# Decoder trunk on one core: the order of the first loads and casts is changed

## The chip, the core and the metric

The kernel runs on one core of a Trainium2 chip. The core has five engines that each run their own list of instructions in order and wait for one another by semaphores: TensorE (matrix products), VectorE, ScalarE, GpSimd and SyncE, which here does nothing but issue the DMAs. The metric is the device time of one launch in microseconds (us).

## The reference

Two layers over 512 tokens of 1024 features. Layer 0 mixes the tokens by causal forgetting attention (16 heads of 64), layer 1 by a short gated convolution. What the change touches is the start of layer 0:

```python
h = rmsnorm(x, norm_pre[i])                       # fox_mixer:
proj = h @ w_in                                   # columns: q | k | v | z | f
f_logit = proj[..., 4 * ATTN_WIDTH:] + b_f
log_f = jax.nn.log_sigmoid(f_logit)
# fox_attention: c = cumsum(log_f)
# logit[t, s] = q_t.k_s / sqrt(Dh) + c[t] - c[s], causal; softmax; times v
return (o * jax.nn.silu(z)) @ w_out
# then x = x + rmsnorm(y, norm_post[i]); x = x + sigmoid(rmsnorm(x, pe_norm[i]) @ pe_w_gate[i]) * (p[i] @ pe_w_proj[i])
```

## The kernel before

**Numbers in two parts.** Every float32 operand of a large product is split into a high part, rounded to the format that TensorE takes (`act_hi`, `w_hi`, `q_hi` and so on), and a low part, what the rounding left (`act_lo`, `w_lo`). A product is then three matmuls into one PSUM bank: high weight by high activation, high weight by low activation, low weight by high activation (`products`, L1028 to L1030). The features lie on the partitions: x is eight tiles of 128 features by 512 tokens.

**Weights come in slots.** A slot is 128 columns of a weight matrix over all 1024 rows, 512 KB. SyncE loads it into one of two raw buffers (`w_raw`, `load_slot`); ScalarE rounds it to the high part (`weight_hi`, L468); GpSimd subtracts to get the low part in four pieces (`weight_lo`, L408), counts `w_ready` up, and so frees the raw buffer for the slot after the next. High and low parts lie in a ring of four. Slots 0 to 3 are q, k, v and z of the first pair of heads, slots 4 to 7 those of the second pair, and so on.

**The prologue.** For each tile of x ScalarE makes `act_hi` (L487) and some of the squares for the norm (L490), VectorE `act_lo` (L728), the other squares (L732), and sums of two squares (L735). TensorE multiplies each tile by the weights of the forget gates (L1052, L1053) and the squares, singly or as sums of two, by a matrix of 1/1024 for the mean (L1062). The norm's scale `rs` is applied only behind the projections. ScalarE and VectorE then make the running sum of the forget gates; SyncE stores it in HBM and reads it back broadcast over the partitions as `bias` rows, four DMAs for each of the two heads of a pair (`load_bias`, L327). In the prologue the two sets of bias rows are issued with slot 4 between them. TensorE meanwhile projects slots 0 and 1.

**The turns.** A turn of 16 steps projects one pair of heads (4 slots, 4 steps each) and does the attention of the pair before. Turn 0 only projects, and there slots 2 and 3 are left. Every engine has its own written order of the steps. In turn 0: step 2, 6, 10 on ScalarE are `weight_hi` of slots 3, 4, 5, step 14 of slot 6 behind v's high part; steps 4 and 5 are q's high parts (L564), step 8 k's (L570), step 14 v's (L588). VectorE scales q, k and v at steps 4, 8, 12 (L795), with q's and k's low parts between (L824, L832). TensorE transposes v at step 14 (L1037), in the middle of slot 3. From turn 1 on ScalarE also does the exps of the attention (L524), VectorE the logits and the normalisation (L763, L772), GpSimd adds the causal mask to the bias rows (L416) between the slots' low parts. Behind eight turns comes the output projection, the gate of layer 0, the convolution layer and its tail; the change touches none of it.

Of the kernel before, what the change touches and what calls it, by code (L numbers as in the profile page):

```python
# [24 lines left out]
ACT = mybir.ActivationFunctionType  # L25
# [4 lines left out]
KT = D // P  # L30
# [9 lines left out]
RING = 4  # L40
# [8 lines left out]
STEP_QKVZ = 0  # L49
# [32 lines left out]
V_AT = 14  # L82
# [3 lines left out]
NORM_AFTER = KT - 3  # L86
PAIRED = 6
WARM = 11
# [24 lines left out]
def trunk(nc, xT_in, pT_in, weights, f_in, b_f_in, pre_in, post_in, pe_in, taps_in, outT):  # L113
# [6 lines left out]
    with ctx:  # L120
# [192 lines left out]
        def _(sp):  # L313
# [15 lines left out]
            for k in range(KT):  # L329
                sp.dma_start(xT[:, k, :], xT_in[k]).then_inc(x_loaded[k], 16)  # L330
                if k == 0:
                    sp.dma_start(g_pre[:], pre_in).then_inc(g_loaded[0], 16)
                    sp.dma_start(f_raw[:], f_in).then_inc(f_loaded, 16)
                if k == 1:
                    load_slot(0, 0)
            sp.dma_start(b_f[:], b_f_in).then_inc(g_loaded[1], 16)
            for slot in range(1, 4):
                load_slot(slot, slot)
# [3 lines left out]
            sp.wait_ge(negc_stored, 16)  # L342

            load_bias(0, 0)
            load_slot(4, 4)
            load_bias(0, 1)
            sp.dma_start(g_post[:], post_in).then_inc(g_loaded[2], 16)
            sp.dma_start(g_pe[:], pe_in).then_inc(g_loaded[3], 16)
            sp.dma_start(taps[:], taps_in).then_inc(g_loaded[4], 16)
            for slot in range(5, 10):  # L350
                load_slot(slot, slot)
# [35 lines left out]
        def _(pool):  # L387
# [41 lines left out]

            pool.wait_ge(act_ready, KT - 1)  # L430
            for slot in range(3):
# [29 lines left out]
        def _(act):  # L461
# [22 lines left out]
            for k in range(KT):  # L484

                act.wait_ge(x_loaded[k], 16)
                nc.scalar.activation(act_hi[0][:, k, :], xT[:, k, :], ACT.Copy, scale=g_pre[:, 0, k:k + 1]  # L487
                                     ).then_inc(act_hi_done, 1)
                if k % 2 == 0 or k >= PAIRED:
                    nc.scalar.activation(x_sq[k][:], xT[:, k, :], ACT.Square).then_inc(x_sq_act, 1)  # L490
                if k == 1:
                    weight_hi(0, 0)
            weight_hi(1, 1)

# [20 lines left out]
            act.wait_ge(f_act, 2)  # L515
            nc.scalar.activation(f_ln[:], f_ln[:], ACT.Ln, bias=1.0).then_inc(f_act, 1)
            weight_hi(2, 2)
            nc.scalar.preload_act_table(ACT.Tanh)

# [25 lines left out]
            def turn(m0, jj, project, attend):  # L545
# [3 lines left out]
                for g in range(GROUPS):  # L549
# [22 lines left out]
                    if g == WEIGHTS_AT and not project:  # L572
                        weight_hi(SLOT_OUT[0] + 3, SLOT_OUT[0] + 3)
                    if g % 4 == WEIGHTS_AT and project and (attend or g != V_AT):

                        weight_hi(count(3 + g // 4, 4, m0, jj), 3 + 4 * m0 + g // 4)
                    if attend and g in SUM_AT:
                        head_half(SUM_AT[g], m0, jj)
                    if g == V_AT and project:
# [144 lines left out]
        def _(dve):  # L724
            for k in range(KT):
# [295 lines left out]
        def _(pe):  # L1021
# [28 lines left out]
            for k in range(KT):  # L1050
# [4 lines left out]
                if k == KT - 1:  # L1055
                    end.then_inc(f_done, 1)
                if k >= PAIRED:
                    pe.wait_ge(x_sq_act, PAIRED // 2 + k - PAIRED + 1)
                elif k % 2 == 1:
                    pe.wait_ge(x_pair, k // 2 + 1)  # L1060
                if k >= PAIRED or k % 2 == 1:
                    end = nc.tensor.matmul(ps_o[:], mean_f[:], x_sq[k][:], start=k == 1, stop=k == KT - 1)  # L1062
            end.then_inc(ms_done, 1)

            bank = ps_pj[STEP_QKVZ % 2]
            pe.wait_ge(w_hi_done, SLOT_QKVZ + 1)
            for k in range(KT):
                w_h = w_hi[SLOT_QKVZ % RING][:, k, :]
                nc.tensor.matmul(bank[:], w_h, act_hi[0][:, k, :], start=k == 0, stop=False)
                nc.tensor.matmul(bank[:], w_h, act_lo[0][:, k, :], start=False, stop=False)  # L1070
            pe.wait_ge(w_ready, SLOT_QKVZ + 1)
            for k in range(KT):
                end = nc.tensor.matmul(bank[:], w_lo[SLOT_QKVZ % RING][:, k, :], act_hi[0][:, k, :], start=False,
                                       stop=k == KT - 1)
# [212 lines left out]
```

## Time and profile before

| | us |
|---|---|
| median of 3 runs | 659.37 (658.58 to 660.58) |
| the profiled execution, own time | 658.61 |
| its span, first to last instruction | 656.8 |
| TensorE busy in it | 635.0 (97%) |
| VectorE, ScalarE, GpSimd busy | 389.9, 321.2, 308.1 |

Times in the rows are us from the start of the span. Matmuls overlap in the pipeline: one of 128x512 is shown with some 0.39 us, and the next starts 0.23 us behind it. The share of a whole engine is an average; the places where TensorE is not busy have to be read stretch by stretch.

### The profile page before, as it was taken

To read this page: it belongs to the slowest core of one execution; us is meant where nothing else is said; L and a number is where in the kernel's file an instruction comes from. 1 tells how busy PE (TensorE), PEld (TensorE's weight loads), DVE (VectorE), ACT (ScalarE), POOL (GpSimd) and SP (SyncE) were. 2 spreads that over 40 slices of the span, in tenths; PEclk is the share of its full clock that TensorE was granted. 3 is DMA by queue.
4 is the path that set the end of the run, shared out by engine and by line. 5 is a ranking of instruction groups with operands and counts; after the bars stand their busy time and mean duration, and the time that the engine had idled before them with its cause. 6 is when DMAs were issued, how large, how long until landed. Compare 5 with 4: busy or idle time off the path is not lost.

```text
span 656.8 us, 9280 instructions
## 1 busy us (share of the span) xinstructions
PE 635.0 (97%) x2930; PEld 516.4 (79%) x2930; DVE 389.9 (59%) x776; ACT 321.2 (49%) x556; POOL 308.1 (47%) x412
## 2 busy tenths in 40 slices
PE   6979999999999999899989999999999999999897
PEld 3758888888888887788767778888888887887686
DVE  5528787867878787645678735333423343365864
ACT  6536575755656575465547633212222222465461
POOL 1765555556464445200277647547454752001770
PEclk9989999999999999999999999999999999999999
DMA  6253333332433333135002413232223232250041
GB/s 200 88 174 128 127 106 105 104 105 104 129 118 114 111 129 125 33 128 188 6 33 72 150 53 110 98 125 96 96 68 123 96 128 87 94 173 32 33 128 65
DMA packets 27161, 68.69 MB, mean 105 GB/s; under 512 B 3568, under 2 KB 10096, under 8 KB 27136
## 3 DMA queue, kind: packets, MB, share of 16 engines
q1 hardware_dynamic: 27136, 68.37, 31.6%
q8 instruction: 14, 0.23, 0.1%
q14 instruction: 11, 0.09, 0.0%
HBM read 66.23 MB, written 2.13 MB: 104 GB/s over the span
## 4 chain that ended last, share of the span: by engine, by line
PE 81%; DVE 9%; ACT 4%; issue 3%; DMA 2%; SPq 0%; DVEq 0%; ACTq 0%
PE ps_pj L1028 23%; PE ps_pj L1030 23%; PE ps_pj L1029 23%; PE ps_tr L1037 3%; DVE act_lo L918 2%; DMA w_raw<-in_weights 2%; PE ps_o L1141 1%; PE ps_o L1142 1%; DVE xT L914 1%; PE ps_sc L1111 1%; PE ps_sc L1109 1%; PE ps_tr L1028 1%; PE ps_tr L1030 1%; PE ps_tr L1029 1%; ACT logit L524 1%
## 5 line engine op out<-in xcount | busy, mean ns | idle before, releaser
L408 POOL TENSOR_TENSOR w_lo<-w_raw,w_hi 128x256 fp32r<-128x256 f32 x324 | 251.5, 809 | 138.5 <-ACT w_hi L468 128.3
L1028 PE MATMUL ps_pj<-act_hi,w_hi 128*128 128x512 f32 (+1 forms) x736 | 293.9, 399 | 5.5 <-DVE act_lo L918 4.4
L1030 PE MATMUL ps_pj<-act_hi,w_lo 128*128 128x512 f32 (+1 forms) x736 | 286.2, 389 | 0.0
L1029 PE MATMUL ps_pj<-act_lo,w_hi 128*128 128x512 f32 (+1 forms) x736 | 285.9, 388 | 0.0
L1028 PEld LDWEIGHTS ps_pj<-act_hi,w_hi 128*128 128x128 f32 x736 | 138.8, 189 | 37.2 <-DVE act_lo L918 7.9
L1030 PEld LDWEIGHTS ps_pj<-act_hi,w_lo 128*128 128x128 f32 x736 | 138.5, 188 | 29.3
L1029 PEld LDWEIGHTS ps_pj<-act_lo,w_hi 128*128 128x128 f32 x736 | 139.0, 189 | 24.9 <-issue 0.7
L468 ACT CAST w_hi<-w_raw 128x1024 fp32r<-128x1024 f32 x96 | 100.6, 1048 | 97.4 <-DMA w_raw<-in_weights 74.9
L443 POOL TENSOR_TENSOR acc<-acc,sq 128x512 f32<-128x512 f32 x14 | 21.4, 1525 | 118.5 <-ACT sq L616 117.6
L416 POOL TENSOR_TENSOR bias<-bias,future 128x128 f32<-128x128 f32 x64 | 34.0, 562 | 72.8 <-DMA bias<-negc_scratch 72.8
L524 ACT ACTIVATE logit<-logit,nmax 128x128 f32<-128x128 f32 (+1 forms) x64 | 36.1, 564 | 60.4 <-DVE nmax L763 60.2
L778 DVE TENSOR_TENSOR pt_lo<-ps_tr,pt_hi 128x128 fp32r<-128x128 f32 (+1 forms) x64 | 30.7, 483 | 8.1 <-ACT pt_hi L534 7.1
L772 DVE TENSOR_SCALAR logit<-logit,rrec 128x128 f32<-128x128 f32 (+1 forms) x64 | 32.6, 510 | 2.2
L891 DVE TENSOR_TENSOR w_lo<-w_raw,w_hi 128x1024 fp32r<-128x1024 f32 x15 | 18.4, 1225 | 25.5 <-ACT w_hi L468 25.5
L763 DVE CUSTOM_DVE_ANT_0 logit<-ps_sc,bias 128x128 f32<-128x128 f32 (+1 forms) x64 | 31.0, 484 | 0.3
L1037 PE MATMUL ps_tr<-ident,logit 128*128 128x128 f32 x160 | 28.2, 274 | 2.3 <-DVE logit L772 2.2
L1037 PEld LDWEIGHTS ps_tr<-ident,logit 128*128 128x128 f32 x160 | 20.5, 140 | 10.3 <-DVE logit L772 4.2
L1005 DVE TENSOR_TENSOR cv_z<-ps_pj,rs 128x512 f32<-128x512 f32 x8 | 5.5, 691 | 38.0 <-PE ps_pj L1030 38.0
L534 ACT CAST pt_hi<-ps_tr 128x128 fp32r<-128x128 f32 (+1 forms) x64 | 26.4, 423 | 2.4 <-PE ps_tr L1037 1.3
L824 DVE TENSOR_TENSOR q_lo<-scaled,q_hi 64x512 fp32r<-64x512 f32 x32 | 24.8, 776 | 3.4 <-ACT q_hi L564 3.0
L985 DVE TENSOR_TENSOR cv_w<-ps_pj,cv_c 128x512 f32<-128x512 f32 x8 | 5.5, 691 | 31.6 <-PE ps_pj L1030 31.4
L918 DVE SCALAR_TENSOR_TENSOR act_lo<-xT,g_pe,act_hi 128x512 fp32r<-128x512 f32 x16 | 20.9, 1318 | 5.2 <-ACT act_hi L655 5.2
(143 smaller groups left out, 724.8 us busy)
## 6 DMA issues: line engine op xcount, KB each, us to landing
w_raw<-in_weights SPq DMA_DIRECT2D x100, 512.0 KB, 3.4
bias<-negc_scratch SPq DMA_DIRECT2D x16, 256.0 KB, 7.4
bias<-negc_scratch SPq DMA_DIRECT2D x16, 192.0 KB, 6.1
xT<-in_xT SPq DMA_DIRECT2D x8, 256.0 KB, 5.5
bias<-negc_scratch SPq DMA_DIRECT2D x16, 128.0 KB, 4.8
out<-xT SPq DMA_DIRECT2D x7, 256.0 KB, 2.0
bias<-negc_scratch SPq DMA_DIRECT2D x16, 64.0 KB, 3.4
p_in<-in_pT SPq DMA_DIRECT2D x2, 512.0 KB, 4.5
```

The costliest lines, as they stand in the source:

```text
L408: last = nc.gpsimd.tensor_tensor(w_lo[place % RING][:, tiles], w_raw[stream(place) % RAW][:, tiles], w_hi[place % RING][:, tiles], ALU.sub ...
L416: nc.gpsimd.tensor_tensor(diagonal, diagonal, future[:], ALU.add).then_inc(bias_ready[h], 1)
L468: nc.scalar.copy(w_hi[place % RING][:], w_raw[position % RAW][:]).then_inc(w_hi_done, 1)
L524: nc.scalar.activation(logit[b][:, 0:n], logit[b][:, 0:n], ACT.Exp, scale=-1.0, bias=nmax[:, b:b + 1], accum_out=rsum[:, b:b + 1]).then_in ...
L763: nc.vector.tensor_tensor_reduce(out=logit[b][:, 0:n], in0=ps_sc[u % 2][:, 0:n], in1=bias[h][:, i, 0:n], scale=-1.0, scalar=3e38, op0=ALU. ...
L772: nc.vector.tensor_scalar(logit[b][:, 0:n], logit[b][:, 0:n], rrec[:, b:b + 1], None, ALU.mult).then_inc(prob_ready, 1)
L778: nc.vector.tensor_tensor(causal(pt_lo, i), ps_tr[n % TR_BANKS][:, 0:(i + 1) * P].rearrange("p (k c) -> p k c", c=P), causal(pt_hi, i), AL ...
L918: nc.vector.scalar_tensor_tensor(a_g[1][:, m - 1, :], xT[:, m - 1, :], g_pe[:, l, m - 1:m], a_g[0][:, m - 1, :], ALU.mult, ALU.subtract).t ...
L1028: nc.tensor.matmul(out, w_h, a[0][:, k, tokens], start=k == first, stop=False)
L1029: nc.tensor.matmul(out, w_h, a[1][:, k, tokens], start=False, stop=False)
L1030: end = nc.tensor.matmul(out, w_l, a[0][:, k, tokens], start=False, stop=k == last)
L1037: last = nc.tensor.transpose(ps_tr[n % TR_BANKS][:, t * P:(t + 1) * P], tile, ident[:])
```

## The change

SyncE issues the eight tiles of x first, then the forget bias, then slots 0 to 3; slot 0 stood behind tile 1. Behind the store of the forget sums, slot 4 is issued ahead of the first set of bias rows, and slots 5 and 6 between the two sets; 4 stood between the sets, and 5 and 6 behind both. ScalarE squares tiles 0, 1, 2, 4, 6 and 7 and VectorE tiles 3 and 5 (before, VectorE had 1, 3 and 5), so that TensorE's mean has six products and not five. `weight_hi` of slot 0 goes behind all of x, that of slot 1 behind the norm's scale, that of slot 2 behind the load of the tanh table. In turn 0, q's, k's and v's high parts go ahead of slot 3, of slot 4 and of slots 5 and 6. GpSimd's first low part waits for eight tiles of `act_lo` and not seven. TensorE projects slot 1 as it did slot 0: all products with the high part first, then those with the low part.

```diff
-PAIRED = 6
+PAIRED = {2: 3, 4: 5}
+MEANS = [k for k in range(KT) if k not in PAIRED]
+TURN_0_WEIGHTS = {5: [0], 8: [1], 14: [2, 3]}
@@ SyncE
-                if k == 1:
-                    load_slot(0, 0)
             sp.dma_start(b_f[:], b_f_in).then_inc(g_loaded[1], 16)
-            for slot in range(1, 4):
+            for slot in range(4):
                 load_slot(slot, slot)
...
+            load_slot(4, 4)
             load_bias(0, 0)
-            load_slot(4, 4)
+            load_slot(5, 5)
+            load_slot(6, 6)
             load_bias(0, 1)
...
-            for slot in range(5, 10):
+            for slot in range(7, 10):
                 load_slot(slot, slot)
@@ GpSimd
-            pool.wait_ge(act_ready, KT - 1)
+            pool.wait_ge(act_ready, KT)
@@ ScalarE
-                if k % 2 == 0 or k >= PAIRED:
+                if k not in PAIRED.values():
                     nc.scalar.activation(x_sq[k][:], xT[:, k, :], ACT.Square).then_inc(x_sq_act, 1)
-                if k == 1:
-                    weight_hi(0, 0)
-            weight_hi(1, 1)
+            weight_hi(0, 0)
...
             norm_scale(0, rs[:])
+            weight_hi(1, 1)
...
+            nc.scalar.preload_act_table(ACT.Tanh)
             weight_hi(2, 2)
-            nc.scalar.preload_act_table(ACT.Tanh)
...
-                    if g % 4 == WEIGHTS_AT and project and (attend or g != V_AT):
+                    if g % 4 == WEIGHTS_AT and project and attend:
...
-                        if not attend:
-                            weight_hi(3 + g // 4, 3 + g // 4)
+                    if not attend:
+                        for j in TURN_0_WEIGHTS.get(g, []):
+                            weight_hi(3 + j, 3 + j)
@@ VectorE
-                if k % 2 == 1 and k < PAIRED:
+                if k in PAIRED.values():
@@ TensorE (the second slot of the first projection)
-            pe.wait_ge(w_ready, SLOT_QKVZ + 2)
-            for k in range(KT):
-                end = products(ps_pj[(STEP_QKVZ + 1) % 2], SLOT_QKVZ + 1, act0, [k], 0, KT - 1)
+            for j in range(2):
+                bank, place = ps_pj[(STEP_QKVZ + j) % 2], (SLOT_QKVZ + j) % RING
+                pe.wait_ge(w_hi_done, SLOT_QKVZ + j + 1)
...
+                pe.wait_ge(w_ready, SLOT_QKVZ + j + 1)
```

SyncE behind the first four slots, before. `w_raw0` and `w_raw1` are the two raw buffers, and the number behind `bias` is the head of the pair:

```order
L341 DMA negc_scratch<-f_abs 16x512 [waits f_chain]
L327 DMA bias0<-negc_scratch 128x128 [waits negc_stored]
L327 DMA bias0<-negc_scratch 128x256
L327 DMA bias0<-negc_scratch 128x384
L327 DMA bias0<-negc_scratch 128x512
L319 DMA w_raw0<-in_weights 128x1024 [waits w_ready]
L327 DMA bias1<-negc_scratch 128x128
```

and now:

```order
L341 DMA negc_scratch<-f_abs 16x512 [waits f_chain]
L321 DMA w_raw0<-in_weights 128x1024 [waits w_ready,negc_stored]
L329 DMA bias0<-negc_scratch 128x128
L329 DMA bias0<-negc_scratch 128x256
L329 DMA bias0<-negc_scratch 128x384
L329 DMA bias0<-negc_scratch 128x512
L321 DMA w_raw1<-in_weights 128x1024 [waits w_ready]
L321 DMA w_raw0<-in_weights 128x1024 [waits w_ready]
L329 DMA bias1<-negc_scratch 128x128
```

Slot 4 (the first `w_raw0` of each) moved from behind four bias rows to ahead of them, and slots 5 and 6 came in ahead of the second set.

ScalarE before, from where the norm's scale `rs` is made. `w_hi0` stands for slots 0, 4, 8, `w_hi1` for slots 1, 5 and so on:

```order
L500 ACTIVATE rs<-ln_ms 128x512 [waits ln_done]
L512 ACTIVATE f_abs<-f_x1,b_f 16x512 [waits f_scaled,g_loaded1]
L514 ACTIVATE f_ln<-f_abs 16x512 [waits f_act]
L516 ACTIVATE f_ln<-f_ln 16x512 [waits f_act]
L468 CAST w_hi2<-w_raw0 128x1024 [waits w_loaded0]
L518 ACT_TABLE_LOAD
L468 CAST w_hi3<-w_raw1 128x1024 [waits w_loaded1]
L564 CAST q_hi00<-scaled0 64x512 [waits pj_free0]
...
L468 CAST w_hi0<-w_raw0 128x1024 [waits pj_done,w_loaded0]
L570 CAST k_st00<-scaled1 64x512 [waits pj_free1]
L570 CAST k_st01<-scaled1 64x512
```

and now:

```order
L500 ACTIVATE rs<-ln_ms 128x512 [waits ln_done]
L470 CAST w_hi1<-w_raw1 128x1024 [waits w_loaded1]
...
L518 ACT_TABLE_LOAD
L470 CAST w_hi2<-w_raw0 128x1024 [waits w_loaded0]
L565 CAST q_hi00<-scaled0 64x512 [waits pj_free0]
...
L470 CAST w_hi3<-w_raw1 128x1024 [waits w_loaded1]
L571 CAST k_st00<-scaled1 64x512 [waits pj_free1]
L571 CAST k_st01<-scaled1 64x512
L470 CAST w_hi0<-w_raw0 128x1024 [waits pj_done,w_loaded0]
```

The cast of slot 4 (`w_hi0` here) moved from ahead of k's high parts to behind them, slot 3's from ahead of q's to behind, and the table load from behind slot 2's cast to ahead of it.

## Rows read from the trace of the kernel before

**Rows 1.** Windows of TensorE: stretch, length, busy (instructions), granted clock, DMA share, GB/s.
```profile
38.20:42.30 4.10, 0.00 (x0) 1.00 0.77 184
42.30:46.00 3.70, 3.67 (x11) 0.54 0.41 149
...
47.20:255.00 207.80, 207.63 (x1061) 1.00 0.35 114
```

**Rows 2.** Waits of TensorE, all of the span: us in total, times, longest.
```profile
PE ps_tr L1037 <- DVE scaled L795: 4.1, 1, 4.1
```

**Rows 3.** Chain of work that ended last: start us, us, what.
```profile
24.70 2.83 DMA negc_scratch<-f_abs
...
29.34 7.97 DMA w_raw<-in_weights
```

**Rows 4.** Timeline of TensorE: start us, us, instruction.
```profile
18.57 0.80 PE L1069 MATMUL ps_pj<-act_hi,w_hi 128*128 128x512 f32 x1
...
29.88 0.39 PE L1028 MATMUL ps_pj<-act_hi,w_hi 128*128 128x512 f32 x1
...
37.81 0.39 PE L1030 MATMUL ps_pj<-act_hi,w_lo 128*128 128x512 f32 x1
42.33 0.90 PE L1037 MATMUL ps_tr<-ident,scaled 128*128 128x128 f32 x4 [4.13 <-DVE scaled L795]
...
47.19 0.22 PE L1109 MATMUL ps_sc<-k_st,q_hi 128*128 128x128 f32 x1
...
52.13 0.27 PE L1037 MATMUL ps_tr<-ident,logit 128*128 128x128 f32 x1
...
73.74 0.62 PE L1037 MATMUL ps_tr<-ident,scaled 128*128 128x128 f32 x4
...
76.94 0.22 PE L1109 MATMUL ps_sc<-k_st,q_hi 128*128 128x128 f32 x1
```

**Rows 5.** Timeline of ScalarE; in brackets, idle time before and its releaser.
```profile
4.83 0.72 ACT L487 ACTIVATE act_hi<-xT,g_pre 128x512 fp32r<-128x512 f32 x1
...
5.98 0.71 ACT L487 ACTIVATE act_hi<-xT,g_pre 128x512 fp32r<-128x512 f32 x1
7.59 1.05 ACT L468 CAST w_hi<-w_raw 128x1024 fp32r<-128x1024 f32 x1 [0.91 <-DMA w_raw<-in_weights]
8.54 0.72 ACT L487 ACTIVATE act_hi<-xT,g_pre 128x512 fp32r<-128x512 f32 x1
...
23.27 1.03 ACT L468 CAST w_hi<-w_raw 128x1024 fp32r<-128x1024 f32 x1
...
48.33 0.40 ACT L524 ACTIVATE logit<-logit,nmax 128x128 f32<-128x128 f32 x1 [1.85 <-DVE nmax L763]
...
52.80 1.04 ACT L468 CAST w_hi<-w_raw 128x1024 fp32r<-128x1024 f32 x1
...
345.68 1.28 ACT L678 ACT_TABLE_LOAD   x1
346.98 0.63 ACT L698 ACTIVATE t_b<-t_a 128x512 f32<-128x512 f32 x1
```

**Rows 6.** Timeline of VectorE.
```profile
15.22 1.41 DVE L728 SCALAR_TENSOR_TENSOR act_lo<-xT,g_pre,act_hi 128x512 fp32r<-128x512 f32 x2
...
49.06 0.86 DVE L772 TENSOR_SCALAR logit<-logit,rrec 128x128 f32<-128x128 f32 x1
```

**Rows 7.** Timeline of GpSimd.
```profile
24.37 6.62 POOL L408 TENSOR_TENSOR w_lo<-w_raw,w_hi 128x256 fp32r<-128x256 f32 x8 [1.68 <-ACT w_hi L468]
38.47 3.67 POOL L408 TENSOR_TENSOR w_lo<-w_raw,w_hi 128x256 fp32r<-128x256 f32 x4 [7.48 <-ACT w_hi L468]
```

**Rows 8.** DMAs issued at 3.07, 57.0 and 58 to 59.5: KB, us to landing.
```profile
xT<-in_xT SPq DMA_DIRECT2D x1, 256.0 KB, 5.2
...
w_raw<-in_weights SPq DMA_DIRECT2D x1, 512.0 KB, 3.5
...
bias<-negc_scratch SPq DMA_DIRECT2D x1, 256.0 KB, 6.8
```

**Rows 9.** Windows of the DMA engines: stretch, length, clock, share, GB/s.
```profile
8.00:9.00 1.00, 1.00 1.02 365
```

More of the change, by code:

```diff
@@ L730, in _ @@
                                                ).then_inc(act_ready, 1)
-                if k % 2 == 1 and k < PAIRED:
+                if k in PAIRED.values():
+                    pair = list(PAIRED.values()).index(k)
                     nc.vector.tensor_tensor(x_sq[k][:], xT[:, k, :], xT[:, k, :], ALU.mult).then_inc(x_sq_dve, 1)
-                    dve.wait_ge(x_sq_act, k // 2 + 1)
-                    dve.wait_ge(x_sq_dve, k // 2 + 1)
+                    dve.wait_ge(x_sq_act, k - pair)
+                    dve.wait_ge(x_sq_dve, pair + 1)
                     nc.vector.tensor_tensor(x_sq[k][:], x_sq[k - 1][:], x_sq[k][:], ALU.add).then_inc(x_pair, 1)
@@ L1056, in _ @@
                     end.then_inc(f_done, 1)
[L1057 to L1062, printed above, removed]
-            end.then_inc(ms_done, 1)
-            bank = ps_pj[STEP_QKVZ % 2]
-            pe.wait_ge(w_hi_done, SLOT_QKVZ + 1)
@@ L1067, in _ @@
-            for k in range(KT):
[L1068 to L1074, printed above, removed]
@@ L1075, in _ @@
-            end.then_inc(pj_done, 1)
-            pe.wait_ge(w_ready, SLOT_QKVZ + 2)
-            for k in range(KT):
-                end = products(ps_pj[(STEP_QKVZ + 1) % 2], SLOT_QKVZ + 1, act0, [k], 0, KT - 1)
-            end.then_inc(pj_done, 1)
+                summed = sum(paired < k for paired in PAIRED.values())
+                if k in PAIRED.values():
+                    pe.wait_ge(x_pair, summed + 1)
+                elif k not in PAIRED:
+                    pe.wait_ge(x_sq_act, k - summed + 1)
@@ new lines, in _ @@
+                if k in MEANS:
+                    end = nc.tensor.matmul(ps_o[:], mean_f[:], x_sq[k][:], start=k == MEANS[0], stop=k == KT - 1)
+            end.then_inc(ms_done, 1)
+            for j in range(2):
+                bank, place = ps_pj[(STEP_QKVZ + j) % 2], (SLOT_QKVZ + j) % RING
+                pe.wait_ge(w_hi_done, SLOT_QKVZ + j + 1)
+                for k in range(KT):
+                    nc.tensor.matmul(bank[:], w_hi[place][:, k, :], act_hi[0][:, k, :], start=k == 0, stop=False)
+                    nc.tensor.matmul(bank[:], w_hi[place][:, k, :], act_lo[0][:, k, :], start=False, stop=False)
+                pe.wait_ge(w_ready, SLOT_QKVZ + j + 1)
+                for k in range(KT):
+                    end = nc.tensor.matmul(bank[:], w_lo[place][:, k, :], act_hi[0][:, k, :], start=False,
+                                           stop=k == KT - 1)
+                end.then_inc(pj_done, 1)
```

## The prediction

> **What bounds the kernel now.** Read the windows of TensorE first. From 47.2 to 255 us it is busy for 207.63 of 207.80 us [rows 1], so in the attention turns nothing but TensorE's own work sets the time. What an edit of the prologue can gain is what lies in front of 47.2 us, and it is kept if the turns behind stay full. Next the list of TensorE's waits: one entry stands out, 4.1 us before the four transposes of v [rows 2]. The windows around it show nothing running from 38.2 to 42.3, and then a granted clock of 0.54 from 42.3 to 46.0, that is mostly 1.2 GHz where 2.4 had been granted [rows 1]. So the gap costs twice: by itself, and by half speed behind it.
>
> Then the chain, to see what the gap waited for. It runs through the load of the raw weights of slot 4, 7.97 us from issue at 29.34 to landing [rows 3]. ScalarE's order has w_hi of slot 4 ahead of k's high parts; VectorE makes k's low parts before it scales v; TensorE needs scaled v for its transposes. A weight that is first used in turn 1 thereby holds a step of turn 0. In the same place of turn 1 a weight load that has no bias rows ahead of it lands in 3.5 us, and the bias rows issued behind it in 6.8 [rows 8].
>
> The start of the stream is a second place. ScalarE is idle 0.91 us at 7.59, waiting for slot 0's weights, then rounds them for 0.95 us while x tile 2 waits [rows 5]; everything up to TensorE's first projection at 18.57 [rows 4] hangs on this.
>
> **The change part by part.**
>
> *x first, six squares on ScalarE.* Before, ScalarE reaches tile 2 at 8.54. A tile's high part and its square take it 1.15 us (tile 0: 4.83 to tile 1 at 5.98 [rows 5]). After, tile 1 has both, and ScalarE is at tile 2 at 5.98 + 1.15 = 7.12. From tile 2 to 7 the order on ScalarE and VectorE is the same before and after (pairs 2/3 and 4/5 stay on VectorE), so tiles 2 to 7 come **1.42 us** earlier. The pair 0/1 leaves VectorE, two instructions fewer; TensorE has one mean product more, at about 8 us, where it waits for tiles anyway: nothing. The loads must keep up: x tile 2, issued at 3.07, landed 5.2 later, at 8.3 [rows 8]; half a MB of weights less ahead of it is 1.4 us at 365 GB/s [rows 9], so 6.9, in time for 7.12. The tiles behind it come 0.7 us apart at that rate and ScalarE needs 0.9 for one. Slot 0's weights come last, by about 11.6, and are wanted at 12.9 (behind tile 7) and by TensorE at 17.1. The last two act_lo, 15.22 to 16.63 [rows 6], end at 15.2; there GpSimd, which now waits for the eighth instead of the seventh, begins slot 0's low part, done by 18.6 and wanted at 21.2. First projection: 18.57 − 1.42 = 17.15.
>
> *w_hi of slot 1 behind the norm's scale, table load ahead of w_hi 2.* The casts use no time of TensorE as long as they are there: slot 1's high part is wanted at 23.0 and is ready by 20.0; its low part is wanted 16 products later, at 26.6 (this is what the split of slot 1 into high then low products is for), and is ready by 23.4. In the forget gates' chain w_hi 1 fits into a wait for VectorE; I add 0.1 at most. Behind that chain's last activation w_hi 2 started at 23.27 [rows 5]; ScalarE is now there at 21.95. Then the table load comes first, 1.30: w_hi 2 starts at 23.25, as before, while TensorE is 1.42 early: slot 2 started at 29.88 [rows 4], after 28.46. GpSimd's four subtractions for slot 2 start at 24.3. Eight of them at 24.37 took 6.62, so four 3.3; beside VectorE's work on k four took 3.67 [rows 7], and q's low parts now run beside them from 25.6. I take 3.6, near the slower row: ready at 27.9, **margin 0.6 us**, cost nothing. Between 3.3 and 3.67 (27.6 to 28.0) it stays nothing; 4.1 would still fit.
>
> Here a rule speaks against the change. The rows: an activation behind a table load starts 1.30 us after the load does, 345.68 to 346.98 [rows 5]. The Trainium skill (ScalarE: Activation LUTs, "What ACT_TABLE_LOAD costs") gives 1.28 for the load and 1.38 for a drain, 2.66 in all; by that rule slot 2's low part would be ready 1.36 later and TensorE would stand still for 0.8. The trace does not agree with it, and the sum goes by the row.
>
> *Slot 3 and q.* w_hi 3 now comes behind q's high parts, at 26.7, when its load lands too (GpSimd frees the buffer at about 23.4). Its low part is done at about 31.4 and wanted at 33.9.
>
> *Slot 4 ahead of the bias rows.* SyncE's store of the forget sums took 2.83 us from 24.70 to landing [rows 3]; after, it goes out at about 23.8, behind slot 3's load, and is done by 27. Slot 4 waits for GpSimd's slot 2, 27.9, so the bias rows are issued from 28.35, 0.8 later than before. They are first wanted in turn 1. Slot 4 lands at 27.9 + 3.5 = 31.4. k's high parts need it no more: they stand ahead, at 30.2, when VectorE is through with q's low parts and scales k. k's low parts end by 33.5, v is scaled at 34.6 and TensorE wants it at 38.04 − 1.42 = 36.6 (last product 37.81 + 0.23 [rows 4]). **The wait at 42.33 is gone**: 42.33 − 38.04 = 4.29. From the first transpose to the first score of the next turn it is 47.19 − 42.33 = 4.86 us at half speed, and in turn 1, warm, 76.94 − 73.74 = 3.20 [rows 4]: **1.66** more.
>
> *What is late next.* Slots 5 and 6 are now rounded one after the other behind v's high parts, ahead of turn 1's first exp. Slot 5 is issued at about 31.4 behind bias row 0, which by the turn 1 pattern lands 6.8 after its last issue at 29.7 [rows 8]: 36.5, and the weights 1.4 behind, 37.9; v is through at 37.8. Slot 6 waits for slot 4's subtractions (w_hi 31.4 to 32.4, 3.67 for four: 36.1) and lands 3.5 behind that at 39.6. w_hi 6 ends at 40.6. Turn 1 begins at 36.6 + 3.2 = 39.8, and its first exp is wanted 1.14 later (48.33 − 47.19), at 40.95 [rows 5]. It fits by 0.3. Behind it, slot 7 is issued at 42.2 behind bias row 1 and lands at about 45.4, where ScalarE wants it at 52.80 − 7.4 = 45.4 [rows 5]. If one is late, TensorE has slack: the first probabilities, done at 49.92 [rows 6], are taken at 52.13 [rows 4]: 2.2 us.
>
> **The sum.** 1.42 + 4.29 + 1.66 = 7.4 us. The profiled execution took 658.6 us at a span of 656.8, and its span becomes **649.4**, its own time 651.2. The median of the runs shown, 659.37, lies 0.8 above it: forecast **651.9**. All that is behind 47.2 only moves.
>
> **The rivals.** *A. The stall moves to turn 1.* Slots 5, 6 or 7 come later, because each now stands behind a set of bias rows with a slow read; slot 4, in that place, took 8 us. If slot 7 takes 8 from 42.2 it lands at 50.2 and not 45.4; of that TensorE's slack takes some 2, and 2.8 us remain, up to 1.7 more if the clock falls as it did behind 4.1 us of nothing: 654.7 to 656.4. Against it: in turn 1 the order weights, bias, weights shows no TensorE wait.
> *B. The x tiles don't come sooner.* If the weights weren't what delayed them, ScalarE has tile 2 only at 8.3 and the first term shrinks to 0.2: 653.1. For it, a tile takes 5.2 us to land even at a high rate; against it, slot 0's half MB lies ahead of tile 2 in the order of issue.
> *C. Slot 2's low part is late.* The table load holds w_hi 2 for its own length, 1.28, once more; ready at 29.2 and not 27.9, a stall of 0.7: 652.6. Against it: 345.68 to 346.98 [rows 5]. This is the drain of the Trainium skill's page named above.
> *D. Slower.* w_hi 6 stands ahead of the first exp on ScalarE, and nothing passes it. Were slot 6 so late that turn 1 stood still for longer than was gained, the kernel would lose: w_hi 6 has to end 2.2 + 7.4 + 2 − 1.7 = 9.9 us behind 40.95, so slot 6 would have to land at 49.8, 13.7 us after its issue, for 661.4. The load of slot 4 took 7.97 [rows 3].
> *E. The change does nothing*: v still waits, say because bias rows issued later hold slot 4; only if the loads don't start in the order of issue. Gain 1.4, 658.0.
>
> **How the numbers follow.** Forecast with all three terms, 0.68 (that includes C's small stalls up to 0.3); A 0.14; B 0.07; C 0.07; D 0.02; E 0.02. The range from 650.6 (0.5 below the sum for the spread of the runs and a clock that recovers sooner, and 0.8 for a prologue that moves more than 1.42) to 655.2 holds the forecast, B, C and the lower part of A. About 0.3%, 2 us, is what a measurement of this kernel can tell from no change. Faster by more than that: forecast, B, C and nearly all of A, 0.94; within it: E and the worst of A, 0.04; slower: D, 0.02.
>
> **What the profile after would show.** TensorE's first projection at 17.1 to 17.2; slot 2 without a wait at 28.5; no entry of 4 us before the transposes of v, which start at 36.6; a granted clock of 1.00 throughout 38 to 46; turn 1's first score at 39.8; slot 4 landing within 4 us, slots 5 and 6 by 38.5 and 40. A would show as a wait of TensorE at the transposes of turn 1 behind w_hi 6 or 7 that waits for a load; B as ScalarE idle on x tiles; C as a wait at slot 2's first product. I am wrong if turns behind 47.2 show gaps that they did not have, or if another wait takes the place at 36.6.

## The result and the profile after

The changed kernel takes **652.09 us** (median of 4 runs, 651.79 to 652.51) against 659.35 us for the kernel before (4 runs, 658.58 to 660.58) on the same chip: a ratio of 0.9885, with a 95% interval of 0.9862 to 0.9907. The profiled execution took 651.79 us at a span of 650.0.

The windows of TensorE come first again (stretch, length, busy and instructions, granted clock, DMA share, GB/s). They answer to [rows 1]:

```profile
38.20:46.00 7.80, 7.80 (x39) 1.00 0.74 189
40.00:248.00 208.00, 207.27 (x1058) 1.00 0.38 116
```

Where TensorE did nothing for 4.1 us and then ran at a clock of 0.54, it is now busy throughout at 1.00. But the long stretch behind it, which was full to 0.17 us, now has 0.73 us of nothing in it. In the list of TensorE's waits the entry before the transposes of v [rows 2] is gone; of those behind the prologue these are left (us in total, times, longest):

```profile
PE ps_pj L1031 <- DVE act_lo L921: 4.4, 6, 1.1
PE ps_tr L1040 <- DVE logit L775: 2.3, 3, 0.9
```

TensorE's timeline has the first projection, slot 2, the transposes of v and the first scores of turns 1 and 2, for which [rows 4] has 18.57, 29.88, 42.33, 47.19 and 76.94:

```profile
17.35 0.80 PE L1073 MATMUL ps_pj<-act_hi,w_hi 128*128 128x512 f32 x1
...
28.66 0.39 PE L1031 MATMUL ps_pj<-act_hi,w_hi 128*128 128x512 f32 x1
...
36.82 0.60 PE L1040 MATMUL ps_tr<-ident,scaled 128*128 128x128 f32 x4
...
40.01 0.22 PE L1109 MATMUL ps_sc<-k_st,q_hi 128*128 128x128 f32 x1
...
62.82 0.66 PE L1040 MATMUL ps_tr<-ident,logit 128*128 128x128 f32 x4 [0.48 <-DVE logit L775]
...
66.47 0.50 PE L1141 MATMUL ps_o<-pt_hi,v_st 128*128 128x512 f32 x1 [0.23 <-DVE pt_lo L781]
...
71.00 0.22 PE L1109 MATMUL ps_sc<-k_st,q_hi 128*128 128x128 f32 x1
```

Turn 1 starts 7.18 us earlier, turn 2 only 5.94. The 1.24 between them is lost late in turn 1, at the two waits in brackets: compared with the kernel before, each counted from the turn's first score, TensorE is 0.03 behind just ahead of the first and 1.2 behind after the second. The brackets hold 0.71 of it, the rest is the slower run of the matmuls on either side of a wait. ScalarE's timeline shows what the engine waits for on the way there (answering to [rows 5]):

```profile
7.34 0.71 ACT L489 ACTIVATE act_hi<-xT,g_pre 128x512 fp32r<-128x512 f32 x1
...
22.12 1.28 ACT L518 ACT_TABLE_LOAD   x1
...
23.42 1.05 ACT L470 CAST w_hi<-w_raw 128x1024 fp32r<-128x1024 f32 x1
...
39.44 1.05 ACT L470 CAST w_hi<-w_raw 128x1024 fp32r<-128x1024 f32 x1 [1.33 <-DMA w_raw<-in_weights]
40.72 1.05 ACT L470 CAST w_hi<-w_raw 128x1024 fp32r<-128x1024 f32 x1 [0.24 <-DMA w_raw<-in_weights]
41.67 0.40 ACT L525 ACTIVATE logit<-logit,nmax 128x128 f32<-128x128 f32 x1
...
47.11 1.06 ACT L470 CAST w_hi<-w_raw 128x1024 fp32r<-128x1024 f32 x1 [0.95 <-DMA w_raw<-in_weights]
```

The casts of slots 5, 6 and 7 (39.44, 40.72, 47.11) each wait for a load. SyncE's issues show what stands ahead of them (start, length of the group of issues; the two of the last row start at 31.99 and 36.11):

```profile
24.53 0.43 SPq L341 DMA_DIRECT2D negc_scratch<-f_abs  x1
28.36 0.33 SPq L321 DMA_DIRECT2D w_raw<-in_weights  x1
28.73 1.85 SPq L329 DMA_DIRECT2D bias<-negc_scratch  x4
31.99 4.45 SPq L321 DMA_DIRECT2D w_raw<-in_weights  x2
```

Slot 4, with nothing ahead of it, landed 3.2 us behind its issue; slot 5, behind the four DMAs of the first set of bias rows, 7.4. The last of these four took, in KB and us from issue to landing:

```profile
bias<-negc_scratch SPq DMA_DIRECT2D x1, 256.0 KB, 8.0
```

It was issued at 30.15 and landed at 38.11, and slot 5 landed 1.3 behind it, at 39.41.

**A measure that is cleaner than the median.** In what follows each kernel's start is read at two landmarks, the first score of turn 1 and that of turn 2, and the rest is the span less the second. All come from the timelines and spans of the profiled executions, one for each kernel. None of these edits touches anything in the rest. The landmark has its own noise: the change, profiled twice, has turn 2 at 71.00 and at 70.38, and the kernel of e7 and e11 at 70.31 and 70.56. So a difference under some 0.6 us at turn 2 is not shown by one trace of each. The kernel before was profiled once.

| kernel | median | before, same chip | turn 1 at | turn 2 at | rest |
|---|---|---|---|---|---|
| before | 659.35 | | 47.19 | 76.94 | 579.9 |
| the change | 652.09 | 659.35 | 40.01 | 71.00 | 579.0 |
| e1 loads only | 651.40 | 657.27 | 41.60 | 71.38 | 578.4 |
| e2 casts only | 655.41 | 657.27 | 41.12 | 73.93 | 579.7 |
| e3 loads and casts | 651.88 | 657.27 | 41.15 | 71.11 | 579.4 |
| e4 start only | 658.39 | 657.27 | 47.32 | 77.07 | 578.7 |
| e5 gap filled | 655.50 | 658.12 | 45.23 | 74.95 | 578.2 |
| e6 table load behind | 651.77 | 658.12 | 40.02 | 70.57 | 579.6 |
| e7 slot 1 early | 651.57 | 658.12 | 39.81 | 70.31 | 578.4 |
| e8 only slot 4 ahead | 654.80 | 658.12 | 40.11 | 75.00 | 578.6 |
| e9 start and loads | 651.68 | 657.59 | 41.84 | 71.56 | 579.6 |
| e10 the change again | 651.90 | 657.59 | 39.84 | 70.38 | 578.4 |
| e11 slot 1 early again | 651.11 | 657.59 | 39.89 | 70.56 | 578.6 |
| e12 start, slot 1 early | 656.77 | 657.59 | 46.35 | 76.10 | 578.3 |

The rest differs by up to 1.7 us between executions that do the same work there. One part of that is where the attention ends. TensorE's timeline and windows there in e9 (rest 579.6), then the windows in e7 (rest 578.4):

```profile
256.06 0.55 PE L1038 MATMUL ps_tr<-ident,logit 128*128 128x128 f32 x3 [0.90 <-DVE logit L773]
258.46 1.11 PE L1038 MATMUL ps_tr<-ident,logit 128*128 128x128 f32 x4 [1.16 <-DVE logit L773]
```

```profile
256.00:260.00 4.00, 2.79 (x13) 0.79 0.01 2
260.00:264.00 4.00, 4.00 (x17) 0.78 0.37 131
...
258.50:261.50 3.00, 3.00 (x11) 0.50 0.16 41
```

```profile
256.00:260.00 4.00, 2.85 (x18) 1.00 0.10 17
260.00:264.00 4.00, 4.00 (x23) 1.00 0.29 114
```

Both kernels wait there; in some executions the clock falls behind the waits and in others it doesn't. The 0.79 and 0.78 are one fall, seen in two windows: between 258.5 and 261.5 the clock is 0.50, that is 1.2 GHz. Of the six longest rests, e3, e6 and e9 (579.4 to 579.6) have such a fall; before, the change and e2 (579.0 to 579.9) don't. These three are slower in the turns: from the first score of turn 2 to that of turn 8 it takes 179.15, 178.74 and 179.59 us, and 178.3 to 178.5 in the other eleven. The runs of the kernel before that stand beside e9 and e10 have spans of 654.3 to 656.7, on the whole the longer the lower their mean clock (0.997 down to 0.991). So medians tell apart some 1 to 2 us, and only the landmarks can speak of less.

### The profile page after: what moved, and what is told of

Its sections match the earlier page's. It is cut to its first block, busy times and chain, and to the rows that moved or that the text cites. A ratio compares the mean times of both kernels' runs of the same rounds, so it can differ in the third digit from the quotient of the medians.

```text
span 650.0 us, 9283 instructions
## 1 busy us (share of the span) xinstructions
PE 633.4 (97%) x2932; PEld 515.5 (79%) x2932; DVE 388.8 (60%) x774; ACT 321.3 (49%) x557; POOL 308.0 (47%) x412
## 4 chain that ended last, share of the span: by engine, by line
PE 81%; DVE 8%; ACT 3%; issue 3%; POOL 3%; DMA 1%; SPq 0%; DVEq 0%; POOLq 0%; ACTq 0%
PE ps_pj L1031 23%; PE ps_pj L1033 23%; PE ps_pj L1032 23%; PE ps_tr L1040 3%; POOL w_lo L410 2%; DVE act_lo L921 2%; PE ps_o L1141 1%; PE ps_o L1142 1%; DVE xT L917 1%; PE ps_sc L1111 1%; PE ps_sc L1109 1%; PE ps_tr L1031 1%; PE ps_tr L1033 1%; PE ps_tr L1032 1%; ACT logit L525 1%
## 5 line engine op out<-in xcount | busy, mean ns | idle before, releaser
L1031 PE MATMUL ps_pj<-act_hi,w_hi 128*128 128x512 f32 (+1 forms) x728 | 290.0, 398 | 5.5 <-DVE act_lo L921 4.4
L1033 PE MATMUL ps_pj<-act_hi,w_lo 128*128 128x512 f32 (+1 forms) x728 | 282.6, 388 | 0.0
L1032 PE MATMUL ps_pj<-act_lo,w_hi 128*128 128x512 f32 (+1 forms) x728 | 282.3, 388 | 0.0
L1031 PEld LDWEIGHTS ps_pj<-act_hi,w_hi 128*128 128x128 f32 x728 | 136.8, 188 | 36.7 <-DVE act_lo L921 7.9
L1033 PEld LDWEIGHTS ps_pj<-act_hi,w_lo 128*128 128x128 f32 x728 | 136.7, 188 | 28.6
L1032 PEld LDWEIGHTS ps_pj<-act_lo,w_hi 128*128 128x128 f32 x728 | 137.0, 188 | 24.7 <-issue 0.7
```

Source lines behind the costliest of these rows:

```text
L1031: nc.tensor.matmul(out, w_h, a[0][:, k, tokens], start=k == first, stop=False)
L1032: nc.tensor.matmul(out, w_h, a[1][:, k, tokens], start=False, stop=False)
L1033: end = nc.tensor.matmul(out, w_l, a[0][:, k, tokens], start=False, stop=k == last)
```

## The experiments

**e1: only SyncE's order behind the forget sums.** Against the kernel before:

```
-            load_bias(0, 0)
             load_slot(4, 4)
+            load_bias(0, 0)
+            load_slot(5, 5)
+            load_slot(6, 6)
             load_bias(0, 1)
...
-            for slot in range(5, 10):
+            for slot in range(7, 10):
```

> The kernel before, with only the loads of slots 4 to 6 reordered (slot 4 ahead of the first bias rows, 5 and 6 between the sets); casts and prologue as before. Theory: slot 4's late load is what held k's high parts, so the wait before v's transposes goes even with the old cast order: slot 4 lands at about 31, v is scaled at 36.9, wanted at 38.04. Gain 4.3 + 1.7 = 6.0 us, time 653.4, turn 1's first score at 41.2. Rival (the cast order is what counts, a load in front of k's casts still holds them): a wait of 1 us or more remains before v's transposes, time over 655.

651.40 us (4 runs) against 657.27 (16 runs), ratio 0.9912 (0.9897 to 0.9927). TensorE's transposes of v start at 38.41 without a wait, though ScalarE still rounds slot 4 ahead of k's high parts:

```profile
31.44 1.05 ACT L470 CAST w_hi<-w_raw 128x1024 fp32r<-128x1024 f32 x1 [1.61 <-DMA w_raw<-in_weights]
33.52 1.25 ACT L572 CAST k_st<-scaled 64x512 fp32r<-64x512 f32 x2 [1.02 <-DVE scaled L797]
38.99 1.05 ACT L470 CAST w_hi<-w_raw 128x1024 fp32r<-128x1024 f32 x1 [4.23 <-DMA w_raw<-in_weights]
```

Slot 4 was there at 31.4, and k's high parts wait for VectorE and no longer for a load. Moving the three loads is enough by itself. The gain was put at 6.0 us and is 5.9.

**e2: only ScalarE's order in turn 0**, with the loads as late as before. Against the kernel before:

```
+TURN_0_WEIGHTS = {5: [0], 8: [1], 14: [2, 3]}
-                    if g % 4 == WEIGHTS_AT and project and (attend or g != V_AT):
+                    if g % 4 == WEIGHTS_AT and project and attend:
-                        if not attend:
-                            weight_hi(3 + g // 4, 3 + g // 4)
+                    if not attend:
+                        for j in TURN_0_WEIGHTS.get(g, []):
+                            weight_hi(3 + j, 3 + j)
```

> The kernel before, with only turn 0's casts reordered on ScalarE (q, k, v ahead of slots 3, 4, 5 and 6); loads and prologue as before. Theory: the wait before v's transposes goes too (k is cast at 33), but slots 4 to 6 land as late as before (37.3, 43, 45), so slot 4's low part is 0.7 us late for turn 1 and slot 6's cast holds the first exp by some 4 us, of which 2.2 are slack: a gain of 6.0 less 2.6, time 656, more if the clock falls again. Rival (only the cast order matters): 653.4.

655.41 us (5 runs) against 657.27, ratio 0.9966 (0.9953 to 0.9979). The wait at v is gone here too (37.94), and turn 1 starts at 41.12, but the weights come as late as before. ScalarE, casts of slots 4, 5, 6:

```profile
36.86 1.05 ACT L469 CAST w_hi<-w_raw 128x1024 fp32r<-128x1024 f32 x1 [4.92 <-DMA w_raw<-in_weights]
...
42.47 1.05 ACT L469 CAST w_hi<-w_raw 128x1024 fp32r<-128x1024 f32 x1 [3.25 <-DMA w_raw<-in_weights]
43.95 1.05 ACT L469 CAST w_hi<-w_raw 128x1024 fp32r<-128x1024 f32 x1 [0.44 <-DMA w_raw<-in_weights]
```

Slot 6 is rounded until 45.0, ahead of turn 1's first exp, and turn 1 takes 32.81 us from first score to first score where before took 29.75. Of 6.1 us gained at turn 1, half is paid back: this is rival A, in a kernel where it does happen. Slot 4's low part was expected 0.7 us late for turn 1; no such wait shows. At turn 2 the trace is 3.0 us ahead of before; the medians, 1.9 apart, show less, and this execution's rest is among the longest.

**e3: both**, that is the change without its new start.

> The kernel before with both reorderings of turn 0 (loads of slots 4 to 6 and casts), the prologue as before, which is the change without its start. Theory: 6.0 us, time 653.4, the same as the loads alone. Rival (both orders are needed): at least 1 us below the kernel with the loads alone.

651.88 us (4 runs), ratio 0.9915 (0.99 to 0.9931): the same as e1. In the trace turn 2 starts at 71.11, 0.27 earlier than in e1, which is within the noise of the landmark.

**e4: only the new start** (turn 0's loads and casts as before). Against the change:

```
-            load_slot(4, 4)
             load_bias(0, 0)
-            load_slot(5, 5)
-            load_slot(6, 6)
+            load_slot(4, 4)
             load_bias(0, 1)
...
-            for slot in range(7, 10):
+            for slot in range(5, 10):
```

and e2's edit undone.

> The kernel after with turn 0's loads and casts put back as before, so only the start is changed (x first, six squares, places of the casts of slots 0 to 2 and of the table load, slot 1's products). Additive theory: TensorE's first projection at 17.35 and 1.2 us gained at the end, time 658.1. Rival: the end of the wait at v hangs on SyncE's store of the forget sums, which stands behind slot 3's load and so goes out only 0.2 us earlier; then TensorE comes 1.2 us earlier and waits 1.0 longer: gain 0.2, time 659.1, wait at v of about 5.1.

658.39 us (11 runs), ratio 1.0015 (1.0006 to 1.0024): no gain at all, rather 1.1 us lost. SyncE's list of e4, and below it TensorE's wait:

```profile
18.70 6.18 SPq L320 DMA_DIRECT2D w_raw<-in_weights  x2
24.93 0.43 SPq L340 DMA_DIRECT2D negc_scratch<-f_abs  x1
28.02 1.75 SPq L328 DMA_DIRECT2D bias<-negc_scratch  x4
29.82 0.43 SPq L320 DMA_DIRECT2D w_raw<-in_weights  x1
```

```profile
42.48 0.77 PE L1036 MATMUL ps_tr<-ident,scaled 128*128 128x128 f32 x4 [4.64 <-DVE scaled L794]
```

TensorE starts its first projection at 17.74, 0.83 us earlier than before, and waits 0.5 longer for v, which is scaled no sooner. The store of the forget sums stands behind slot 3's load, which needs slot 1's raw buffer free; slot 1 is now rounded behind the norm's scale, so the store still goes out at 24.9 (24.70 before, [rows 3]), the bias rows at 28.0, slot 4 at 29.8.

**e12: e4 with slot 1 rounded right behind slot 0**, to test that reading. Against e4:

```
             weight_hi(0, 0)
+            weight_hi(1, 1)
...
             norm_scale(0, rs[:])
-            weight_hi(1, 1)
```

> Only the start changed, as in the run of the start alone, but slot 1's cast directly behind slot 0's. Theory: the start alone gave nothing because slot 1's low part ended at 24.5, slot 3's load and the store of the forget sums behind it left late (24.93) and the bias rows at 28.02, so v was released no sooner; now the store leaves at 23.5, bias rows at 26.4, v's transposes start near 41.1: 1.2 us below the kernel before. Rival (the start gives nothing for another reason): no gain again.

656.77 us (11 runs) against 657.59 (15 runs), ratio 0.999 (0.998 to 1.0). The store goes out at 24.09, the bias rows at 26.93, v's transposes start at 41.50 and turn 1 at 46.35, 0.97 earlier than in e4. That fits the chain from slot 1's buffer to slot 4; by time it is worth 0.8 of a microsecond and not the 1.2 expected, at the edge of what the runs tell apart.

**e5: the wait stays, the idleness goes.** The kernel before, with 17 matmuls that nothing reads, ahead of v's transposes (added work: its output is not part of the result).

```
                     if g == V_AT and project:
+                        if not attend:
+                            for _ in range(17):
+                                nc.tensor.matmul(ps_tr[1][:], w_hi[3][:, 0, :], act_hi[0][:, 0, :], start=True, stop=True)
```

> The kernel before with 17 matmuls of 128x512 into an unused bank ahead of turn 0's transposes of v (17 x 0.227 = 3.9 us of the 4.3 us gap); their result is used nowhere. Theory: the wait itself stays, the clock does not fall behind it: granted clock 1.00 from 42 to 46, turn 1's first score 1.7 us earlier (45.5), time 657.7. Rival (the slow stretch has another cause than the idle time): no change, 659.4.

655.50 us (7 runs) against 658.12 (10 runs), ratio 0.9968 (0.9948 to 0.9987). A kernel with more work is faster. TensorE's timeline, then the window behind the gap, of e5 and of before:

```profile
37.79 4.01 PE L1094 MATMUL ps_tr<-act_hi,w_hi 128*128 128x512 f32 x17
41.97 0.66 PE L1037 MATMUL ps_tr<-ident,scaled 128*128 128x128 f32 x4 [0.17 <-DVE scaled L795]
...
45.23 0.22 PE L1112 MATMUL ps_sc<-k_st,q_hi 128*128 128x128 f32 x1
```

```profile
42.00:46.00 4.00, 4.00 (x21) 1.00 0.42 131
```

```profile
42.00:46.00 4.00, 3.67 (x11) 0.57 0.40 145
```

In the same 4 us, 21 matmuls at a clock of 1.00 and 11 at 0.57. From the first transpose of v to turn 1's first score it takes 45.23 − 41.97 = 3.26 us, against 4.86 in before [rows 4]: the clock costs 1.60 us, and the forecast had 1.66. (Turn 2 starts 1.99 earlier; 0.36 of it is that v is transposed earlier in this execution. The medians are 2.6 apart, 0.9 more than was expected; what the 0.6 beyond the trace are is open.) This execution has a fall of its own that before doesn't have, in the prologue:

```profile
8.00:12.00 4.00, 3.28 (x7) 0.68 1.02 396
```

The idle times of TensorE ahead of it, 0.39, 0.37 and 0.72 us, are those of the kernel before (0.50, 0.38 and 0.72), where the clock stayed at 1.00. So the length of the stop alone doesn't tell whether the clock falls.

**e6: the table load behind slot 2's cast.** Against the change:

```
-            nc.scalar.preload_act_table(ACT.Tanh)
             weight_hi(2, 2)
+            nc.scalar.preload_act_table(ACT.Tanh)
```

> The kernel after with the tanh table's load put back behind slot 2's cast. Theory: slot 2's low part is ready 0.4 us ahead of TensorE in the kernel after, so an earlier cast gives nothing: 652.1, slot 2's subtractions at 24.2 and not 24.54, since slot 1's end there. Rival (the load costs TensorE something where it stands): over 0.5 us faster.

651.77 us (4 runs), ratio 0.99 (0.9881 to 0.9919); turn 2 at 70.57. The place of the table load makes no difference that the runs can show.

**e7 and e11: the change with slot 1 rounded early** (e12's edit, made in the changed kernel).

> The kernel after with slot 1's cast directly behind slot 0's, where ScalarE is idle from 14.1 to 17.1. Theory: GpSimd ends slot 1 at 21.5 and not 24.1, slot 3 lands at about 25 and not 27.5, the store goes out 0.9 earlier, slot 5 is issued 0.4 us earlier; the waits of ScalarE for slots 5 to 7 shrink, and the 0.7 us that TensorE loses at the end of turn 1 go in part: 0.3 to 0.7 us faster, 651.4 to 651.8. Rival (these waits are all within slack): 652.1.

> The kernel after with slot 1's cast directly behind slot 0's, on the same chip as the kernel after. Theory: 0.3 to 0.7 us faster than it, the 0.5 and 0.2 us waits in turn 1 gone. Rival: no difference.

651.57 us (4 runs) against 658.12, ratio 0.9899 (0.988 to 0.9917), and on another chip 651.11 (4 runs) against 657.59, ratio 0.9907 (0.9889 to 0.9924), beside the change itself (e10) at 651.90. The store goes out at 23.46 in e7, but slot 4 at 28.38 and no sooner, since its raw buffer has to be freed by slot 2's subtractions, and turn 2 starts at 70.31 and 70.56 against 70.38 in e10. The medians lean by 0.8 us to the edit, the landmarks by nothing: not shown to be better.

**e8: only slot 4 ahead of the bias rows**, slots 5 and 6 behind both sets. Against the change:

```
             load_bias(0, 0)
-            load_slot(5, 5)
-            load_slot(6, 6)
             load_bias(0, 1)
...
-            for slot in range(7, 10):
+            for slot in range(5, 10):
```

> The kernel after with slots 5 and 6 loaded behind both sets of bias rows, as before the change; only slot 4 stands ahead. Theory: slot 5 lands near 44 and slot 6 near 46, ScalarE has to cast both ahead of turn 1's first exp, wanted at 41; with 2.2 us of slack TensorE stands still for about 3 us in turn 1, more with the clock: 655 to 657. Rival (only slot 4's place mattered): 652.1.

654.80 us (4 runs) against 658.12, ratio 0.9945 (0.9926 to 0.9964): half of the gain. Turn 1 starts as early as in the change (40.11), and then the first probabilities are late. ScalarE's casts of slots 5 and 6, and TensorE's first transposes of turn 1:

```profile
43.82 1.05 ACT L468 CAST w_hi<-w_raw 128x1024 fp32r<-128x1024 f32 x1 [5.61 <-DMA w_raw<-in_weights]
45.10 1.04 ACT L468 CAST w_hi<-w_raw 128x1024 fp32r<-128x1024 f32 x1 [0.23 <-DMA w_raw<-in_weights]
```

```profile
47.17 0.33 PE L1038 MATMUL ps_tr<-ident,logit 128*128 128x128 f32 x1 [1.96 <-DVE logit L773]
```

and the windows of TensorE around it:

```profile
44.00:47.00 3.00, 1.21 (x6) 1.00 0.04 15
48.50:51.50 3.00, 3.00 (x9) 0.50 0.52 180
```

The clock falls again, behind a stop of 1.96 us. Turn 1 takes 34.89 us and not 30.55 (e6), so slots 5 and 6 between the two sets are worth 4.4 us in the trace (75.00 − 70.57, e6) and 3.0 by the medians of e6 and e8, which ran on the same chip; e6's profiled rest, with a fall of the clock in it, is 1.0 longer.

**e9: the change with turn 0's casts as before**, and **e10: the change again**, on the same chip.

> The change with turn 0's casts as before: slot 3 ahead of q's high parts, slot 4 ahead of k's, slot 5 ahead of v's. Theory: with the new start slot 3 lands only at 27.5, so q's high parts begin at 28.5 and not 24.4, VectorE scales v at about 37.7, wanted at 36.8: a wait of some 1 us before v's transposes, about 1 us above the kernel after. Rival (the order of the casts is immaterial once slot 4 lands early, as it was with the old start): the same time as the kernel after within 0.3 us, no wait.

> The change as it is, again, so that it shares a chip with the three below. Theory: the start is worth 1.2 us only where the loads of slots 4 to 6 are reordered as well; so about 7 us below the kernel before here, where the loads and casts without the start gave 5.4 and the start alone nothing. Rival (the start gives nothing at all): 5.5 to 6.

e9: 651.68 us (4 runs), ratio 0.9906 (0.9891 to 0.9922). e10: 651.90 (4 runs), ratio 0.9914 (0.9899 to 0.9929). By time they are the same. In the trace e9 waits twice in turn 0, for 0.65 and 0.59, where a single wait of some 1 us was expected, and reaches turn 1 at 41.84, 2.0 later than e10; at turn 2 it is 1.18 later. Where did 0.8 of the 2.0 go? Slot 7's cast on ScalarE, in e10, e9, e3 and e1, in that order, and each kernel's turn 1 began at 39.84, 41.84, 41.15 and 41.60:

```profile
46.68 1.05 ACT L470 CAST w_hi<-w_raw 128x1024 fp32r<-128x1024 f32 x1 [1.30 <-DMA w_raw<-in_weights]
```

```profile
47.13 1.04 ACT L469 CAST w_hi<-w_raw 128x1024 fp32r<-128x1024 f32 x1
```

```profile
47.18 1.04 ACT L471 CAST w_hi<-w_raw 128x1024 fp32r<-128x1024 f32 x1
```

```profile
47.04 1.04 ACT L470 CAST w_hi<-w_raw 128x1024 fp32r<-128x1024 f32 x1
```

The turns begin 2.0 us apart, slot 7 is rounded within 0.5. Likewise the first exp of the next head starts at 52.83, 53.64, 53.54 and 53.42. ScalarE and VectorE keep the time of the loads, and TensorE, once it has used up its slack, waits for them: from first score to first score turn 1 takes 29.72 us in e9 and 29.78 in e1, 29.96 in e3, but 30.54 in e10 and 30.99 in the change. In the profiled executions e9 is 2.4 us behind e10, 1.18 of them at turn 2 and 1.2 in the rest, where e9's clock fell; e9's other three runs (651.05 to 651.72) are level with e10's four (650.64 to 652.17). So the medians don't show the 1.18, and with one trace of e9 it isn't shown that the order of the casts is worth it.

## Why the prediction was right, and where it was not

The forecast was 651.9 us and the measurement 652.09; the likeliest case came true, by the cause that it named. That the two agree to 0.2 us is luck: the gain behind the wait was put about 1 us too high, and what made up for it is no work of the change. Step by step:

- **The wait at v, 4.29, and the half clock behind it, 1.66.** Both confirmed. e1 removes both with the loads alone (turn 1 5.59 earlier, turn 2 5.56), and e5 removes the clock's part alone: 1.60.
- **The order of causes.** The prediction gave the wait to slot 4's load and ScalarE's order together. e1 and e2 show that either one cures it. But the loads cure it for good, and the casts alone move half of it to turn 1.
- **The start, 1.42.** The first projection came at 17.35, not 17.15. Tile 2 moved from 8.54 to 7.34, that is 1.20 and not 1.42, since the whole of ScalarE's list began 0.24 later, on a forget weight that landed later. In e10, on another chip, the first projection came at 17.18. This term failed more at its other end. It was added whole, as if everything moved with it. e4 shows 0 for it alone, since slot 4 does not move; in the full change it brings turn 1 forward by 1.1 to 1.3 (e3 against the change and e10) and turn 2 by 0.1 to 0.7. The mis-sized step is "slot 7 is issued at 42.2 behind bias row 1 and lands at about 45.4, where ScalarE wants it": it was issued at 43.41 and landed at 47.1 (46.65 in e10), 1.7 late, and turn 1 lost 1.24 against [rows 4]. ScalarE's fourth exp of the head stands behind that cast and comes 8.22 us behind the turn's first score, 7.00 before; TensorE's first wait is for what comes of the next head's fourth exp, 20.76 behind and not 19.48. In the five profiles of the change and its small variants the cast starts at 46.66, 46.68, 46.86, 46.88 and 47.11 (e7, e10, e11, e6, the change) and turn 2 at 70.31, 70.38, 70.56, 70.57 and 71.00. That is rival A, in small, on top of the forecast. The text had said that all behind 47.2 only moves; 1.24 us of it did not.
- **Why the number came out all the same.** The span fell by 6.8, of which 5.94 stand at turn 2. The other 0.86 is the rest (579.9 to 579.0), which no edit explains. So of 7.4 us forecast, some 6 to 6.6 are the change's (76.94 − 71.00, 76.94 − 70.38), and on another chip, where before takes 657.6, the same change gains 5.7. The forecast of 7.4 was too large by about 1 us, and the rest of before on the first chip, the longest in the table, filled that in. The profiled execution was forecast at 651.2 and took 651.79; the median stood 0.3 above it and not the 0.8 that was added. (659.37 less the three terms is 652.0; the forecast has 651.9.)
- **The store, forecast for 23.8, went out at 24.53.** Slot 3's load holds it until slot 1's low part is done (24.13). The prediction named the queue ("behind slot 3's load") but had slot 1 ready at 23.4; its four subtractions took 3.90 us, and 3.4 were allowed. Three of them took 0.73 to 0.89 and the last 1.66, beside VectorE's running sum of the forget gates. GpSimd and VectorE:

```profile
22.47 1.66 POOL L410 TENSOR_TENSOR w_lo<-w_raw,w_hi 128x256 fp32r<-128x256 f32 x1
```

```profile
22.21 1.38 DVE L750 TENSOR_TENSOR_SCAN f_abs<-f_ln,f_min 16x512 f32<-16x512 f32 x1 [1.69 <-ACT f_ln L517]
```

All six profiles with slot 1's cast behind the norm's scale have this one of 1.65 or 1.66. With slot 1 rounded early (e7, e11, e12) the subtractions are through before the sum starts, none takes more than 1.19, and in e7 the store goes out at 23.46.
- **Slot 2's low part, margin 0.6**: it was done at 28.27 and wanted at 28.66, a margin of 0.39, no wait. GpSimd, answering to [rows 7], slots 1 and 2:

```profile
20.23 3.90 POOL L410 TENSOR_TENSOR w_lo<-w_raw,w_hi 128x256 fp32r<-128x256 f32 x4 [1.95 <-ACT w_hi L470]
24.54 3.73 POOL L410 TENSOR_TENSOR w_lo<-w_raw,w_hi 128x256 fp32r<-128x256 f32 x4 [0.41 <-ACT w_hi L470]
```

- **Rival B, x tiles that don't come sooner.** ScalarE is at tile 2 at 7.34 and waits for no load there: it did not occur.
- **Rival C, the table load's drain.** The load starts at 22.12 and the cast behind it at 23.42: 1.30, as the row of before had it, and e6 finds nothing to gain by moving it. The 1.28 us for the load that the Trainium skill (ScalarE: Activation LUTs, "What ACT_TABLE_LOAD costs") gives agrees with this trace; its further 1.38 us of drain does not show.
- **TensorE's slack before the first transposes, 2.2.** e8 measures it: the first exp could have started at about 41.2, when its input was ready, and started behind slot 6's cast at 46.05, 4.8 later, and TensorE waited 1.96: slack 2.8. The point from which rival D would have decided was therefore farther away than worked out.
- **Slots 4 to 6.** Issued at 28.36, 31.99 and 36.11 and there at 31.5, 39.4 and 40.7, against 31.4, 37.9 and 39.6 forecast. The 1.4 us for slot 5's own bytes were right (1.3). What was late is the set of bias rows ahead of it: 38.11 and not 36.5, since its last DMA went out 0.45 later than forecast and took 8.0 us and not 6.8 (6.9 to 8.0 in the profiles with this order of loads). Slot 7 likewise lands 1.5 behind the second set (45.54). In e6 it was issued 1.4 earlier, at 41.99, and landed at 46.86, only 0.2 earlier: the queue ahead of it decides, not its own issue.

What stays open: why the clock falls at the attention's end in some executions only; what lengthens the turns of before, the change and e2 (e4, with the loads and casts of before, takes 178.5 for turns 2 to 7, which speaks against these); why e4's median lies 1.1 above before's where its trace (turn 2 at 77.07) says 0.1; and whether e7's edit is worth anything.

## What to carry to other kernels

Where an engine's work list has a step that waits for a load, ask of each load what the queue must finish ahead of it: moving three loads ahead of slow broadcast reads was worth nearly the whole change (e1), with only the first of them moved half of the gain is gone (e8), and the reordering of casts and the earlier start together brought another 0.4 to 1.0 us at the landmark (71.38 against 71.00 and 70.38), which the medians don't show. A gain at the front of a pipeline is kept only as far as the loads behind come sooner too; look for the first step that stays at its old absolute time, for there the gain ends. Judge edits of a microsecond at a landmark behind which both kernels do the same work, not by the end of the span.

## What the runs showed of the hardware

- A stop of TensorE of 1.96 us was followed by a granted clock of 0.50 (1.2 GHz) from 48.5 to 51.5 in e8. Behind the two stops of 0.90 and 1.16 at the attention's end it stayed at 1.00 in e7 and e10 and was 0.50 from 258.5 to 261.5 in e9; e3 and e6 have such a fall too, the other eleven profiles don't. The prediction had counted on a fall only behind 4.1.
- Filling a stop with matmuls that nobody reads gained 2.6 us by the medians (e5); 1.60 of them the trace shows to be the clock that it kept.
- Reading the forget sums back, broadcast, holds up a 512 KB load that is issued behind it: 7.4 us to landing against 3.2 without (the change; slots 5 and 4). The load lands 1.3 behind the last of the rows.
- GpSimd's subtraction of 128x256 took 0.72 to 0.75 us mostly, 1.19 for some that ran beside VectorE's subtractions of q's low part, and 1.66 for the one that ran beside VectorE's running sum (the change).
